# Sparse attention in a two-block program: the compressed branch as one batch, the full branches as items of two heads

## The reference

```python
d_c = tq[:, None] - cmp_end[None, :]                      # compressed: 31 blocks of 32 keys, one each 16
s_c = einsum('bhgtd,bhcd->bhgtc', qc, k_cmp) + head_bias(d_c)
p_c = masked_softmax(s_c, d_c >= 0)
o_c = einsum('bhgtc,bhcd->bhgtd', p_c, v_cmp)
...                                                       # selected: top 16 of 8 blocks, so all of them
s_s = einsum('bhgtd,bhtkd->bhgtk', qc, k_s) + b_s
p_s = masked_softmax(s_s, (d_s >= 0)[:, :, None])
o_s = einsum('bhgtk,bhtkd->bhgtd', p_s, v_s)
...                                                       # window of 512, so all earlier keys
p_w = masked_softmax(einsum('bhgtd,bhkd->bhgtk', qc, k_w) + head_bias(d_w), m_w)
o_w = einsum('bhgtk,bhkd->bhgtd', p_w, v_w)
return gc[..., 0:1] * o_c + gc[..., 1:2] * o_s + gc[..., 2:3] * o_w
```

## Time and profile before

| | us |
|---|---|
| median of 3 runs | 3193.66 |
| lowest, highest | 3191.53, 3202.86 |
| the profiled execution | 3211.91 |
| its span | 3210.1 |
| busy in the span: TensorE, VectorE, ScalarE, GpSimd | 3085.5, 1510.4, 1146.1, 249.3 |
| mean granted TensorE clock | 0.937 |

### The profile page before, as it was taken

The page is one execution under the profiler, slowest core; times in us unless marked ns, Lnnn a source line. Parts: engine busy times, 40 slices in busy tenths (PEclk is TensorE's granted clock), DMA queues, the critical chain, the costliest instruction groups (busy, mean ns, idle before and its releaser), DMA issues.

```text
span 3210.1 us, 57591 instructions
## 1 busy us (share of the span) xinstructions
PE 3085.5 (96%) x23446; PEld 2804.4 (87%) x23446; DVE 1510.4 (47%) x2084; ACT 1146.1 (36%) x1699; POOL 249.3 (8%) x203
## 2 busy tenths in 40 slices
PE   8999997899999999999998999999999989999998
PEld 7965545778999999999868999999999976699997
DVE  6543335745544264443776444334443333354433
ACT  3333323334332242323664232223343236633221
POOL 2000001201000000000671000000000000000000
PEclk9955568999999999999999999999999989999999
DMA  5310001312333323333212333343333331132332
GB/s 178 99 46 0 0 0 34 119 59 66 105 92 96 108 80 98 91 98 95 72 40 62 97 94 92 103 131 105 96 90 95 95 100 40 42 100 91 98 97 68
DMA packets 74975, 262.75 MB, mean 82 GB/s; under 512 B 8344, under 2 KB 8472, under 8 KB 74704
## 3 DMA queue, kind: packets, MB, share of 16 engines
q1 hardware_dynamic: 69408, 248.93, 25.6%
q10 hardware_dynamic: 4608, 8.39, 0.7%
q0 software_dynamic: 816, 3.36, 0.3%
HBM read 252.24 MB, written 8.41 MB: 81 GB/s over the span
## 4 chain that ended last, share of the span: by engine, by line
PE 77%; DVE 5%; issue 1%; ACT 1%; DMA 0%; POOL 0%; POOLq 0%; DVEq 0%; ACTq 0%; SPq 0%
PE bank L403 67%; PE bank L896 2%; PE bank L914 1%; PE bank L802 1%; DVE w_lo L1417 1%; DVE bank L1880 1%; PE bank L447 1%; PE bank L490 1%; PE bank L944 1%; PE bank L785 1%; PE bank L941 0%; PE bank L899 0%; PE bank L919 0%; PE bank L925 0%; DVE h_lo L1426 0%
## 5 line engine op out<-in xcount | busy, mean ns | idle before, releaser
L403 PE MATMUL bank<-h_hi,w_hi 128*128 128x256 f32 x4720 | 933.0, 279 | 10.4 <-DVE w_lo L1417 7.2
L403 PE MATMUL bank<-h_lo,w_hi 128*128 128x256 f32 x4720 | 925.2, 277 | 0.0
L403 PE MATMUL bank<-h_hi,w_lo 128*128 128x256 f32 x4720 | 925.2, 277 | 0.0
L1417 DVE TENSOR_TENSOR w_lo<-w_raw,w_hi 128x1024 fp32r<-128x1024 f32 x468 | 584.2, 1251 | 383.6 <-ACT w_hi L979 202.6
L403 PEld LDWEIGHTS bank<-h_hi,w_hi 128*128 128x128 f32 x4720 | 716.9, 189 | 23.4 <-issue 19.6
L403 PEld LDWEIGHTS bank<-h_lo,w_hi 128*128 128x128 f32 x4720 | 715.1, 189 | 0.0
L403 PEld LDWEIGHTS bank<-h_hi,w_lo 128*128 128x128 f32 x4720 | 715.0, 188 | 0.0
L979 ACT ACTIVATE w_hi<-w_raw 128x1024 fp32r<-128x1024 f32 x468 | 476.3, 1049 | 261.6 <-PE bank L403 151.4
L1437 DVE TENSOR_TENSOR t<-bank,rB 128x512 f32<-128x512 f32 x260 | 179.2, 690 | 522.2 <-PE bank L403 521.9
L403 PE MATMUL bank<-a_hi,w_lo 128*128 128x256 f32 x1716 | 335.8, 277 | 0.0
L403 PE MATMUL bank<-a_hi,w_hi 128*128 128x256 f32 x1716 | 335.7, 277 | 0.0
(11 more groups left out here) (300 smaller groups left out, 3242.7 us busy)
## 6 DMA issues: line engine op xcount, KB each, us to landing
w_raw<-in_w_gu SPq DMA_DIRECT2D x220, 512.0 KB, 3.6
w_raw<-in_w_dn SPq DMA_DIRECT2D x80, 512.0 KB, 3.6
w_raw<-in_w_dn SPq DMA_DIRECT2D x40, 384.0 KB, 3.1
w_raw<-in_w_pw SPq DMA_DIRECT2D x24, 512.0 KB, 3.6
w_raw<-in_w_in SPq DMA_DIRECT2D x22, 512.0 KB, 3.7
w_raw<-in_w_xkv SPq DMA_DIRECT2D x16, 512.0 KB, 3.6
w_raw<-in_w_kv SPq DMA_DIRECT2D x16, 512.0 KB, 3.6
stick_qkv<-t ACTq DMA_DIRECT2D x24, 256.0 KB, 2.1
```

The costliest lines, as they stand in the source:

```text
L403: last = nc.tensor.matmul(dst[:, c:c + HALF], w, o[:, at + c:at + c + HALF], start=start and c == 0, stop=stop, skip_group_check=True)
L1417: V.tensor_tensor(cut(w_lo, slot, UNIT), cut(w_raw, slot, UNIT), cut(w_hi, slot, UNIT).bitcast(f32), sub).then_inc(w_lo_made, 1)
```

## The change

The compressed branch leaves the items and becomes one batch ahead of them. Its scores for all eight heads and four query blocks go to 32 blocks of 32 columns in banks 2 and 3; VectorE adds the bias with eight instructions, takes the maxima and sums of all 32 blocks in one instruction each, and scales all at once; ScalarE makes one exponent. Eight transposes turn it, and four copies of the compressed values, each masked to its own 32 rows (`of_group`), let one product of 512 columns per head add the branch to a group's output.

The other two branches become 32 items (c, qb, br), and one item does both halves. The scores of the halves follow each other into two banks (0 and 1, or 2 and 3), the transposes go to banks 4 and 5, one copy of ScalarE takes both, and in the values step the halves alternate within each key block. Groups c alternate between banks 6 and 7. The exponent is made in place in four slots of `n_p`; the bias is read backwards straight from `toep`, the queries from `qT`, the gates from `gate`. All loops are unrolled; no tile is staged per c. The diff, its core, without the loops that go (L617 to L658 on TensorE, L1101 to L1122 on ScalarE, L1698 to L1734 on VectorE), which stand above:

```diff
-NSA_ITEMS = [(half, qb, br) for half in range(2) for qb in range(TB) for br in range(3)]
+NSA_ITEMS = [(c, qb, br) for c in range(4) for qb in range(TB) for br in (1, 2)]
...
+        def nsa_n(s):
+            return P * (NSA_ITEMS[s][1] + 1)
+        def nsa_p(s, half, n):
+            at = (s % 4) * 2 * S + half * S
+            return n_p[:, at:at + n]
+        def nsa_col(kind, s, half):
+            at = 16 + 8 * kind + 2 * (s % 4) + half
+            return small[:, at:at + 1]
+        cmp_p = n_p[:, 6 * S:8 * S]
...
@@ block.tensor
+                for c in range(4):
+                    for f in range(2):
+                        at = (2 + f) * GW + h * NCMP
+                        last = nc.tensor.matmul(bank[5][32 * c:32 * c + 32, h * DH:(h + 1) * DH], cmp_h[:, at:at + 32], w2(1, f),
+                                                start=f == 0, stop=f == 1, tile_position=(0, 32 * c))
             last.then_inc(cmp_proj, 1)
+            NI = len(NSA_ITEMS)
+            def cmp_scores():
+                pe.wait_ge(cmp_out, 1)
+                for qb in range(TB):
+                    for c in range(4):
+                        for half in range(2):
+                            rs = slice(half * DH, (half + 1) * DH)
+                            at = qb * P + c * 32
+                            last = nc.tensor.matmul(bank[2 + half][:, at:at + NCMP], qT[rs, c * S + qb * P:c * S + (qb + 1) * P],
+                                                    kc[rs, 0:NCMP], start=True, stop=True)
+                last.then_inc(k_qk, 1)
+            def cmp_turn():
+                pe.wait_ge(k_exp, 2)
+                for half in range(2):
+                    for qb in range(TB):
+                        at = half * S + qb * P
+                        last = nc.tensor.transpose(bank[4 + half][:, qb * P:(qb + 1) * P], cmp_p[:, at:at + P], ident)
+                last.then_inc(n_turned, 1)
+            def nsa_scores(s):
+                c, qb, br = NSA_ITEMS[s]
+                for half in range(2):
+                    if s >= 2:
+                        pe.wait_ge(n_add, 2 * (s - 2) + half + 1)
+                    elif s == 1:
+                        pe.wait_ge(k_add, 1 + half)
+                    rs = slice(half * DH, (half + 1) * DH)
+                    nc.tensor.matmul(bank[2 * (s % 2) + half][:, 0:nsa_n(s)], qT[rs, c * S + qb * P:c * S + (qb + 1) * P],
+                                     (kS, kW)[br - 1][rs, 0:nsa_n(s)], start=True, stop=True).then_inc(n_qk, 1)
+            def nsa_turn(s):
+                qb = NSA_ITEMS[s][1]
+                pe.wait_ge(n_pT, s + 1)
+                for half in range(2):
+                    pe.wait_ge(n_scaled, 2 * s + half + 1)
+                    for k in range(qb + 1):
+                        last = nc.tensor.transpose(bank[4 + half][:, k * P:(k + 1) * P], nsa_p(s, half, S)[:, k * P:(k + 1) * P], ident)
+                last.then_inc(n_turned, 1)
+            def nsa_values(s):
+                c, qb, br = NSA_ITEMS[s]
+                first, done = s % 8 == 0, s % 8 == 7
+                pe.wait_ge(n_pT, s + 2)
+                if first and c >= 2:
+                    pe.wait_ge(op_lo, R0["nsa"] + c - 1)
+                for k in range(qb + 1):
+                    for half in range(2):
+                        at = k * 2 * P + (br - 1) * P + half * DH
+                        src = (s % 2) * 2 * S + half * S + k * P
+                        last = nc.tensor.matmul(bank[6 + c % 2][half * DH:(half + 1) * DH, qb * P:(qb + 1) * P], v_nsa[:, at:at + DH],
+                                                pT[:, src:src + P], start=first and k == 0, stop=False, skip_group_check=True)
+                if done:
+                    pe.wait_ge(cmp_out, 2)
+                    for half in range(2):
+                        at = (half * 4 + c) * DH
+                        last = nc.tensor.matmul(bank[6 + c % 2][half * DH:(half + 1) * DH, :], v_cmp[:, at:at + DH],
+                                                pT_cmp[:, half * S:(half + 1) * S], start=False, stop=True, skip_group_check=True)
+                last.then_inc(n_pv, 1)
+            cmp_scores()
+            for s in range(NI + 3):
+                if s < NI:
+                    nsa_scores(s)
+                if s == 1:
+                    cmp_turn()
+                if 0 <= s - 2 < NI:
+                    nsa_turn(s - 2)
+                if s >= 3:
+                    nsa_values(s - 3)
...
@@ block.scalar
+            act.wait_ge(k_add, 4)
+            nc.scalar.activation(cmp_p, cmp_p, ACT.Exp).then_inc(k_exp, 1)
+            NI = len(NSA_ITEMS)
+            for s in range(NI + 5):
+                if s < NI:
+                    for half in range(2):
+                        act.wait_ge(n_add, 2 * s + half + 1)
+                        p = nsa_p(s, half, nsa_n(s))
+                        nc.scalar.activation(p, p, ACT.Exp, scale=-1.0, bias=nsa_col(0, s, half),
+                                             accum_out=nsa_col(1, s, half)).then_inc(n_exp, 1)
+                if s == 1:
+                    act.wait_ge(n_turned, 1)
+                    nc.scalar.activation(pT_cmp[:], banks[1][:, 0:2 * S], ACT.Copy).then_inc(n_pT, 1)
+                r = s - 2
+                if 0 <= r < NI:
+                    act.wait_ge(n_turned, r + 2)
+                    if r >= 2:
+                        act.wait_ge(n_pv, r - 1)
+                    n = nsa_n(r)
+                    dst = pT[:, (r % 2) * 2 * S:(r % 2 + 1) * 2 * S].rearrange("p (h n) -> p h n", n=S)[:, :, 0:n]
+                    nc.scalar.activation(dst, banks[1][:, 0:2 * S].rearrange("p (h n) -> p h n", n=S)[:, :, 0:n], ACT.Copy).then_inc(n_pT, 1)
+                r = s - 4
+                if r >= 0 and r % 8 == 7:
+                    act.wait_ge(n_pv, r + 1)
+                    nc.scalar.activation(cut(h_hi, r // 8), bank[6 + r // 8 % 2][:], ACT.Copy).then_inc(op_hi, 1)
...
@@ block.vector
+            V.tensor_reduce(of_group[:], ident.rearrange("p (c j) -> p c j", j=32), AX.X, add).then_inc(k_group, 1)
             dve.wait_ge(cmp_proj, 1)
             V.tensor_copy(kc[:, 0:NCMP], bank[4][:, 0:NCMP]).then_inc(cmp_out, 1)
-            V.tensor_copy(vc[0:NCMP, :], bank[5][0:NCMP, 0:P]).then_inc(cmp_out, 1)
+            dve.wait_ge(k_group, 1)
+            values = bank[5][:, 0:P].rearrange("p (h d) -> p h d", d=DH)
+            for c in range(4):
+                last = V.tensor_scalar(v_cmp[:].rearrange("p (h c d) -> p h c d", c=4, d=DH)[:, :, c], values, of_group[:, c:c + 1], None, mult)
+            last.then_inc(cmp_out, 1)
             for u in (6, 7, 8, 9):
                 split("cmp", 0, 4, u + 2)
             dve.wait_ge(toep_in, 16)
+            NI = len(NSA_ITEMS)
             def nsa_lo(c):
                 dve.wait_ge(op_hi, R0["nsa"] + c + 1)
+                V.tensor_tensor(cut(h_lo, c), bank[6 + c % 2][:], cut(h_hi, c).bitcast(f32), sub).then_inc(op_lo, 1)
+            def nsa_add(s):
+                c, qb, br = NSA_ITEMS[s]
+                n = nsa_n(s)
                 for half in range(2):
+                    h = c + 4 * half
+                    dve.wait_ge(n_qk, 2 * s + half + 1)
+                    if s >= 3 and half == 0:
+                        dve.wait_ge(n_turned, s - 2)
+                    V.tensor_tensor_reduce(nsa_p(s, half, n), bank[2 * (s % 2) + half][:, 0:n], toep[:, h * S:h * S + n][:, ::-1], -1.0, 3.0e38,
+                                           add, amin, nsa_col(0, s, half)).then_inc(n_add, 1)
+            def nsa_scale(s):
+                c, qb, br = NSA_ITEMS[s]
+                dve.wait_ge(n_exp, 2 * s + 2)
+                at = 32 + 2 * (s % 4)
+                steps.done(V.reciprocal(small[:, at:at + 2], small[:, at - 8:at - 6]))
+                for half in range(2):
+                    p, g = nsa_p(s, half, nsa_n(s)), qb * 24 + half * 12 + c * 3 + br
+                    V.tensor_scalar(p, p, nsa_col(2, s, half), gate[:, g:g + 1], mult, mult).then_inc(n_scaled, 1)
+            blocks = cmp_p.rearrange("p (g j) -> p g j", j=32)
+            def per_block(cols):
+                return cols.unsqueeze(2).to_broadcast([P, 32, 32])
+            most, total, factor_of = (cmp_cols[:, 32 * i:32 * i + 32] for i in range(3))
+            def cmp_add():
+                dve.wait_ge(k_qk, 1)
+                dve.wait_ge(k_clear, 1)
+                for half in range(2):
+                    scores = bank[2 + half][:].rearrange("p (q c j) -> p q c j", c=4, j=32)
+                    bias = toep[:].rearrange("p (h j) -> p h j", j=S)[:, 4 * half:4 * half + 4]
+                    dst = cmp_p[:, half * S:(half + 1) * S].rearrange("p (q c j) -> p q c j", c=4, j=32)
+                    for qb in range(TB):
+                        n = 8 * qb + 7
+                        last = V.tensor_tensor(dst[:, qb, :, 0:n], scores[:, qb, :, 0:n], bias[:, :, 0:97 + P * qb:16][:, :, ::-1], add)
```

(28 more changed lines are left out.)

115 lines of the change are left out of this document (6 added, 109 removed).

## The result

| | before | after |
|---|---|---|
| median of 4 runs, us | 3198.19 | 3056.70 |
| lowest, highest | 3191.53, 3202.86 | 3054.32, 3060.77 |
| the profiled execution | 3211.91 | 3060.77 |
| its span | 3210.1 | 3059.0 |
| mean granted TensorE clock | 0.937 | 0.966 |

The change makes the kernel 4.4% faster: the ratio is 0.956, with an interval from 0.9536 to 0.9584. The forecast was 3046 us and its range 3025 to 3095; its own case, halves side by side at a high clock, is the one that came about. In the tables from here on, one execution of the kernel with all three later edits (3077.01 us) is left out, as it is over 1.5% above the fastest of its kernel and counts as slow.

The account below looks back on a forecast made before the run. TensorE, mostly at 1.2 GHz, bounds the 256.4 us sparse-attention stage. Its end, 195 + 77 + 6 + 10 + 6 = 294 against 441.8 us, saves 148: 3064, scaled by 0.9943 to 3046 us, range 3025 to 3095.

Parts of the forecast that it names:

- its own case: Sparse-attention stage: row and column halves overlap and the clock rises to 2.4 GHz; 3046 us, chance 0.65.
- (e): Work added ahead of the items: the pipeline starts at about 195 us, 10 us later than the old; bounds 6 to 15.
- (b): Paired items on TensorE: both heads' scores and values overlap; 68 us in all at 2.4 GHz, 124 at 1.2 GHz.
- (c): What is late next in the items: ScalarE's copy behind two exponents holds up TensorE's transposes; items take 77 us.
- (d): Ends of a group c: compressed value products 0.85 us and h_hi 0.6, about 1.5 us x 4 = 6 us.
- (g): TensorE's clock starts at 1.2 GHz and rises within the first group: 10 us of excess, bounds 0 and 47.
- the last item: End of the stage: the last item must pass all pipeline steps, some 6 us beyond its period.
- the rival said 11: Scores' row halves don't overlap, clock high: items cost 88 us instead of 77; 3057 us, chance 0.12.
- (PE + C)/2: Cost of an item: half of TensorE's time plus the add, exponents and copy path; 3.34 us for four key blocks.
- my three reasons: Why TensorE's clock would rise in the stage: no compressed items, half as many changes of form, the whole array filled.
- The rival at the low clock: TensorE stays at 1.2 GHz for most of the stage: 107 us less, 3087 us, chance 0.16.
- its smallest terms: Lower bound of the stage: TensorE alone 68, no cold excess, start at 191; another 20 us off, 3025 us.

Follow-up runs that it names:

- all three later edits: Kernel after with ScalarE's copy ahead of the exponents, VectorE's four splits at the stage's end, batch softmax by query block: median 3052.78 us, projection to gates 93.7 us.
- copy first: Kernel after with ScalarE's copy of item s - 2 ahead of item s's two exponents: 3062.2 us, then median 3045.91; projection to gates 96.2, then 98.2 us.

## Why the prediction was right, step by step

| term | predicted | measured | from |
|---|---|---|---|
| (e) pipeline starts at | 195 | 197.1 | first transpose of the batch, L653 |
| (b, c) items | 77 | 76.2 | 4 x 19.04, without the batch; holds the h_hi copies, which (d) counted |
| (d) ends of groups c | 6 | 3.4 | 4 x (19.89 - 19.04) |
| (g) cold clock, and the last item | 10 + 6 | 6.2 | what is left up to 282.9 |
| stage's end | 294 | 282.9 | |
| given back later | 0 | 7.9 | 159.0 - 151.1, of which 5.4 are within the scatter |

**(b)** TensorE's prices held: transposes 1.03 and values 1.02 us for k = 4, scores of k = 1 and 2 at 0.42 and 0.63, all as predicted; for k = 4 the scores take 1.17, not 1.05. The overlap of row halves, for which no row stood, was taken from the nearest case (L606), and that was right: apart, the scores cost 9.8 us more in the periods, where the rival said 11. The Trainium skill, TensorEngine Tiling (Array Packing), section Key Properties, had it that different tiles load and multiply in parallel and that only a change of the tiling mode drains the engine. These runs agree with the first, with starts 7 ns apart for two halves. Of the second they show that a change of form costs time and a change of half does not: from the last transpose to the first value instruction it is 0.20 us (218.443 to 218.646), and 0.11 from one pair of value instructions to the next.

**(c)** is the step that carried the forecast. With TensorE alone the items would take 68 us. I took (PE + C)/2 because ScalarE's copy stands behind two exponents; 76.2 us came out where 77.3 were worked out, the waits name that copy, and moving it took 1.6 us off each period. The copy of 1,024 columns took 1.016 us (predicted 1.07), and the backward read of the bias cost nothing, 689 ns for 512 columns against 0.69 in the earlier trace rows:

```profile
L1760 DVE CUSTOM_DVE_ANT_0 n_p<-bank,toep 128x512 f32<-128x512 f32 x16 | 10.4, 689 | 2.7 <-PE bank L664 2.7
...
L1167 ACT ACTIVATE pT<-bank 128x1024 f32<-128x1024 f32 x8 | 8.1, 1016 | 3.5 <-PE bank L673 3.5
```

**(d)** was sized at 1.5 us for each group. The batch's products take 0.85 of it, as priced; the h_hi copies, priced at 0.6, are in the 76.2 of the items. (b) to (d) together: 83 predicted, 79.6 measured.

**(e)** gave nearly the right start for the wrong reason. I let the batch's chain begin when VectorE is done with its splits. It begins when TensorE is done with the 64 compressed score instructions, 7.04 us, which the prediction did not price at all. That the start came within 2.1 us all the same is luck: VectorE, with splits and filling, is free only 0.5 us sooner (188.02 against 188.47), and taking the splits away brought nothing. The projection in 32-column tiles cost nothing, as taken: 32 instructions in 1.11 us.

**(g)** The size was too high and the reasons were mostly wrong. The clock rose 9.1 us after the pipeline's start and never fell within the stage, so little was lost. Of my three reasons, the compressed items and the filling of the array are refuted (clock 0.56 without the one, 1.00 for 96.6 us without the other), and the number of changes of form is at most half right: it did not bring the clock down. The rival at the low clock had 0.16, and the rule beside it, the Trainium skill's TensorE: Matmul & The Clock Gate, Part 4, that transposes do not count as busy for the clock, would have made it hold. Here 152 of the 592 TensorE instructions from 206.2 to 282.9 us are transposes, about a third of the time of an item of four blocks, and the clock stood at 1.00 from 206.2 to 284.7 us. If they don't count, the rest was enough; no run here tells whether they do.

**The signs that were named**: a stage of about 110 us (96), a clock above 0.85 (0.90), heads' scores within 0.1 us (7 ns), alternating values, waits naming the copy of pT, and a quiet stretch at the start all appeared. VectorE and ScalarE at over 70% holds for the fast part only (70 and 71%); over the whole stage it is 70 and 64%.

**Where the 160 us came from.** Leaving out the compressed items gives 50.4. From the kernel after with halves in one place, which without its batch would stand at about 135.0 - 14.2 = 121 us, to 213.9 is 93 us: pairs, the deeper pipeline over eight banks, and the clock that these let rise and stay. The halves side by side give 30.7, and the batch takes 14.2 back. The run with the halves issued apart (174.8) splits the 93: 40 are the pairing of the halves on TensorE, with the sooner rise of the clock that came with it, and 53 the rest. These are differences between single profiles; the 121 is worked out, not measured, and the pipeline's share and the clock's were not taken apart.

**The point.** The profiled execution was predicted at 3064 us and took 3060.8. The stage was 11 us shorter than worked out, nearly all of it the cold clock and the last item in (g), and 8 us were given back: that the two nearly cancel is luck. Yet the median is 10.7 us above the point. That is the factor: I scaled by 0.9943, the median of before over its profiled execution, but that execution stood further above its median than that of after does (3056.7 to 3060.8, 0.9987). One profiled execution is a poor ruler for half a percent. One sum of the prediction is off without effect: its smallest terms take 9 + 10 + 4 = 23 us off, not 20, which puts the lower bound at 3023.

## What to carry to other kernels

When an engine bounds a stage at a low clock, a change that speeds it up has a second price list: work out the items at the high clock too, and ask which other engine's queue order is late then; here one copy behind two exponents set the period. Two heads of size 64 belong in the two halves of the array, alternating in the queue, for scores and for values alike. And when a chain starts behind several engines, price all of them: the one that seems to be in the way may only be the cover of another.

## What the runs showed of the hardware

- Float32 products on different row halves start 7 ns apart, just as those on different column halves do when they alternate; two heads' scores against 512 keys took 1.17 us at 2.4 GHz.
- TensorE overlaps tiles only over a short stretch of its queue: sixteen value instructions took 1.02 us alternating and 1.51 us half by half. With eight, six and four instructions of one half ahead, the other half began beside the fifth, the third and the first of them.
- 64 score instructions of 31 columns took 7.04 us at 1.2 GHz: their records start in pairs, one of each row half and 7 ns apart, one pair every 0.21 us, each instruction with a weight load of 128 columns beside it. So narrow a product costs what 128 columns cost (0.43 us for the two instructions of a head at that clock); without the alternation it would be twice as much, an estimate from that figure.
- The granted clock stayed at 2.4 GHz for 96.6 us on a stream that used half of the array in scores and values. When it rises after a cold start varies: 27.6 and 30.2 us behind the projection in two profiles of the kernel after and 22.8 and 27.6 in two of copy first, 28.0 with the values' halves in one place, but 58.3 with the scores' and 38.3 with both, and 76.4 with the halves issued apart, although TensorE was busy for 57.9 of the last 58.6 us before that rise. What decides it these runs do not show.
- The same dense code ran at different speed from one execution to the next at a nearly equal granted clock: 2755.3 to 2801.2 us behind the stage at a clock of 0.973 and 0.976. One kernel's executions lay up to 45 us apart, more than the edits of 7 to 12 us that the traces show plainly.
